# Modulation of a two-layer hybrid diffusion backbone: ring slots in column tiles of 512 columns, partial sums added by a selector

## The reference

```python
sh1, sc1, g1, sh2, sc2, g2 = jnp.split(jax.nn.silu(cv) @ w_mod + b_mod, 6, axis=-1)
h  = x * (1 + sc1) + sh1
z  = h @ w_in            # attention 512+128+128, mLSTM 4 x 256 + 16 gates, gMLP 2 x 256
y  = jnp.concatenate([att, m_out, g_out], axis=-1) @ w_out
x  = layer_norm(ALPHA * x + g1 * y, ln1_g, ln1_b)
h2 = x * (1 + sc2) + sh2
x  = layer_norm(ALPHA * x + g2 * (jnp.square(jax.nn.relu(h2 @ w_ff1)) @ w_ff2), ln2_g, ln2_b)
```

## Time and profile before

| what | us |
|---|---|
| median of the three runs shown (3286.88 to 3294.17) | 3290.51 |
| the profiled execution's own time | 3296.62 |
| its span | 3294.6 |
| PE busy in the span | 3089.8 (94%) |
| DVE busy | 1657.8 (50%) |
| ACT busy | 962.8 (29%) |
| POOL busy | 457.7 (14%) |
| mean granted clock of PE | 0.966 of 2.4 GHz |
| modulation slots from the ring | 160 of 256 KB, 2.9 to landing |
| chain that ended last | PE 83%, DVE 6%, issue 3%, DMA 3% |

### The profile page before, as it was taken

The page is one execution under the profiler, slowest core; times in us unless marked ns, Lnnn a source line. Parts: engine busy times, 40 slices in busy tenths (PEclk is TensorE's granted clock), DMA queues, the critical chain, the costliest instruction groups (busy, mean ns, idle before and its releaser), DMA issues.

```text
span 3294.6 us, 44616 instructions
## 1 busy us (share of the span) xinstructions
PE 3089.8 (94%) x17016; PEld 2540.1 (77%) x17016; DVE 1657.8 (50%) x3070; ACT 962.8 (29%) x1886; POOL 457.7 (14%) x600
## 2 busy tenths in 40 slices
PE   5999989998999999999968999899989999999996
PEld 4788845567888888889848888455668998899995
DVE  4447677747333333333484376777473333333337
ACT  3222344534221122111233223445342221212221
POOL 0012333412100000000020023334120000000003
PEclk8999989999999999999979999899999999999998
DMA  5440220022222222220321112200121111111113
GB/s 215 151 130 25 76 76 0 0 67 97 81 75 79 80 84 73 81 88 26 131 87 36 45 24 75 76 0 0 68 100 35 52 35 43 52 39 39 52 32 147
DMA packets 99368, 220.08 MB, mean 67 GB/s; under 512 B 13360, under 2 KB 13936, under 8 KB 98672
## 3 DMA queue, kind: packets, MB, share of 16 engines
q1 hardware_dynamic: 78240, 151.76, 14.6%
q0 software_dynamic: 20944, 65.80, 5.5%
HBM read 191.00 MB, written 26.51 MB: 66 GB/s over the span
## 4 chain that ended last, share of the span: by engine, by line
PE 83%; DVE 6%; issue 3%; DMA 3%; ACT 2%; POOL 1%; DVEq 1%; ACTq 1%; POOLq 1%; SPq 0%
PE ps L1655 22%; PE ps L1658 21%; PE ps L1659 21%; PE ps L1870 5%; PE ps L1841 3%; PE ps L1860 2%; PE ps L1637 2%; PE ps L1861 2%; DVE nm L1418 1%; PE ps L1768 1%; DMA w_raw<-in_w_slots 1%; DMA lnb<-in_ln_gb 1%; DVE w_lo L468 1%; POOLq L537 1%; PE ps L1763 1%
## 5 line engine op out<-in xcount | busy, mean ns | idle before, releaser
L1655 PE MATMUL ps<-hi,w_hi 128*128 128x384 f32 x1584 | 541.1, 342 | 29.4 <-DVEq L406 20.9
L1659 PE MATMUL ps<-hi,w_lo 128*128 128x384 f32 x1584 | 534.7, 338 | 0.0
L1658 PE MATMUL ps<-lo,w_hi 128*128 128x384 f32 x1584 | 534.1, 337 | 0.0
L1655 PE MATMUL ps<-w_hi,f_hi 128*128 128x512 f32 x1152 | 457.9, 397 | 19.4 <-DVE acc L1559 19.4
L1658 PE MATMUL ps<-w_lo,f_hi 128*128 128x512 f32 x1152 | 451.2, 392 | 0.0
L1659 PE MATMUL ps<-w_hi,f_lo 128*128 128x512 f32 x1152 | 450.3, 391 | 0.0
L463 ACT CAST w_hi<-w_raw 128x512 fp32r<-128x512 f32 x368 | 213.3, 619 | 763.9 <-PE ps L1655 716.3
L1559 DVE TENSOR_TENSOR acc<-acc,ps 128x512 f32<-128x512 f32 x288 | 196.2, 686 | 418.7 <-PE ps L1659 418.5
L1655 PE MATMUL ps<-w_hi,hi 128*128 128x512 f32 (+1 forms) x1008 | 388.8, 386 | 6.8 <-ACT stg L756 4.1
L1659 PE MATMUL ps<-w_hi,lo 128*128 128x512 f32 (+1 forms) x1008 | 380.7, 378 | 0.0
L1658 PE MATMUL ps<-w_lo,hi 128*128 128x512 f32 (+1 forms) x1008 | 380.5, 378 | 0.0
(11 more groups left out here) (277 smaller groups left out, 4106.5 us busy)
## 6 DMA issues: line engine op xcount, KB each, us to landing
w_raw<-in_w_slots SPq DMA_DIRECT2D x368, 256.0 KB, 3.3
w_raw<-in_m_slots SPq DMA_DIRECT2D x160, 256.0 KB, 2.9
x_dram<-xr POOLq DMA_DIRECT2D x18, 512.0 KB, 3.1
x1t<-x_dram POOLq DMA_DIRECT2D x6, 1536.0 KB, 14.9
out<-acc POOLq DMA_DIRECT2D x18, 512.0 KB, 3.0
modw<-in_w_mod SPq DMA_DIRECT2D x4, 2048.0 KB, 9.3
acc<-in_x_in SPq DMA_DIRECT2D x3, 1536.0 KB, 16.0
zq_dram<-stg POOLq DMA_DIRECT2D x18, 256.0 KB, 2.4
```

Source lines behind the costliest of these rows:

```text
L1655: mm = pe.matmul(out, a_hi, b_hi, start=first, stop=False)
L1658: pe.matmul(out, a_hi, b_lo, start=False, stop=False)
L1659: return pe.matmul(out, a_lo, b_hi, start=False, stop=last)
```

## The change

Seven edits go together.

1. **Slots in column tiles.** `mod_slots` takes four slots (in projection group 0 two) at a time, waits for all of them and makes one matmul of 512 columns for each, slot k in the strip of partitions 32 (k mod 4). A chunk is then four partial sums, each over two slots.
2. **Selector.** `mod_rows` copies the four strips, 2 x 512 each, to a row buffer; `mod_turn` is four matmuls with the 98 x 128 piece as the stationary side and a selector of two columns as the moving side, which turns and adds the four strips. Every chunk is turned, the gates too. The bias is loaded once as columns (`modbc`) and added in `mod_columns`.
3. **Gates.** Their columns go to `gcol`, one more matmul (`mod_gate`) turns them back into rows, DVE copies those (`mod_gates`), POOL stores them. The wait for those stores (mod_st) stands ahead of the next chunk's copies, from the first gate chunk on.
4. **Places.** Projection groups 0, 1, 2 take 2, 3, 3 chunks; group 0 visits after t = 0 to 7, groups 1 and 2 after t = 1 to 6, with turns after t = 3, 5, 7. In a first product PE visits after blocks 1 and 4, turns after 7, gates after 9; in a second after 4 and 8, 12, 15. DVE copies after hidden(6) or summed(9).
5. **Head.** Four buffers for w_mod, all requested at once; the x rows of tiles 0 to 2 ahead of the first weights, the others behind them; group 0's weights split after tiles 2 and 7, before after 5 and 8.
6. **First normalisation.** ACT applies mean and deviation in one pass (`normal1`); norm weight and bias are folded into the modulation columns (`mixed_columns`, `mixed`), so the transposes no longer wait for the weighted x. DVE weights x (`weighted1`, two passes) behind each of the first nine hidden blocks of piece 0, POOL stores it from there. POOL also forms nmean x rstd (`nbias`). PE's `x_turned` comes one tile sooner (t - 2).
7. **acc.** It is no longer cleared; the first piece copies into it.

The diff, cut to its core (the head's transfers, `mixed_columns`, places in memory and the acc edit are told above):

```diff
-Z_CHUNKS = {0: (0, 1, 2), 1: (3, 4), 2: (5, 6, 7)}
+Z_CHUNKS = {0: (0, 1), 1: (2, 3, 4), 2: (5, 6, 7)}
...
+        selm, gcol = condt[:, 0], sce[:, 0:4]
...
+                    deviation(2 * NT * L + t, t, True)
+                for i, t in enumerate(X1_ORDER):
+                    store1(i, t)
...
+                def normal1(t):
+                    act.wait_ge(S["ln_rstd"], 2 * NT * L + t + 1)
+                    act.activation(x_row(t), x_row(t), ACT.Identity, bias=nbias[:, t:t + 1], scale=rs[:, t:t + 1]).then_inc(S["xn_done"], 1)
+                act.wait_ge(S["mc_done"], L + 1)
                 for t in range(NT):
                     squares(2 * NT * L + t, t, x_row(t), sqr[:].rearrange("p (a b) -> p a b", b=W))
-                    if t == NT - 1:
-                        split_hi(act, L, 7, (S["o_out"], START + 18 * L + 18), range(RAW))
-                    if t >= 4:
-                        modulated(L, t - 4)
-                modulated(L, 5)
-                split_hi(act, L, 7, (S["o_out"], START + 18 * L + 18), range(RAW, SLOTS))
+                    if t:
+                        normal1(t - 1)
+                    if t >= 3:
+                        modulated(L, t - 3)
+                normal1(NT - 1)
                 for t in range(6, NT):
+                    if t < 8:
+                        split_hi(act, L, 7, (S["o_out"], START + 18 * L + 18), range((t - 6) * RAW, (t - 5) * RAW))
                     modulated(L, t)
...
             def mod_rows(m, bank):
                 dve.wait_ge(S["mod_ps"], KT * (m + 1))
-                if m < NCH:
-                    dve.wait_ge(S["mod_b0_ld"], 16)
-                else:
-                    dve.wait_ge(S["mod_b_ld"], 16 * (m - NCH + 1))
-                if m:
-                    before = [n for n in range(m) if kind_of(n) < 2]
-                    dve.wait_ge(S["mod_tp"], len(before))
-                    if kind_of(m - 1) == 2:
-                        dve.wait_ge(S["mod_st"], 64 * (m - len(before)))
-                own(dve)
-                b = modb0[:, m] if m < NCH else modb
+                dve.wait_ge(S["mod_tp"], m)
+                if m in (NCH, 3 * NCH):
+                    dve.memset(mod_place(m)[:], 0.0)
+                    dve.drain()
+                if gates_in(m):
+                    dve.wait_ge(S["mod_st"], 64 * gates_in(m))
                 for j in range(4):
                     r = slice(32 * j, 32 * j + 2)
-                    ins = dve.tensor_tensor(modr[r, :], ps[r, bank, m % NCH * P:(m % NCH + 1) * P], b[r, :], ALU.add)
+                    ins = dve.tensor_copy(mod_place(m)[r, :], ps[r, bank, :])
...
+                    src, b = ps[:, bank, 32 * j:32 * j + 2], modbc[:, 4 * m + j:4 * m + j + 1]
+                    if k == 2:
+                        ins = dve.tensor_scalar(gcol[:, j], src, b, None, ALU.add)
+                    elif j < 2:
+                        ins = dve.tensor_scalar(modc[:, o:o + 5:4], src, b, None, ALU.add)
                     else:
-                        ins = dve.tensor_scalar(modc[:, o:o + 5:4], src, 1.0, None, ALU.add)
+                        ins = dve.tensor_scalar(modc[:, o:o + 5:4], src, b, 1.0, ALU.add, ALU.add)
                 ins.then_inc(S["mod_col"], 1)
+            def mod_gates(m, bank):
+                dve.wait_ge(S["mod_gt"], gates_in(m + 1))
+                dve.tensor_copy(mod_place(m)[0:8, P:2 * P], ps[0:8, bank, P:2 * P]).then_inc(S["mod_gr"], 1)
...
+                modulation((NCH,))
+                modulation((NCH + 1,), True, False)
                 split_lo(dve, L, 1)
+                modulation((NCH + 1,), False)
...
-                for part in range(2):
-                    modulation(1, part)
+                modulation(range(NCH + 2, NCH + 5))
...
+                    if n == 1:
+                        modulation((NCH + 4,), False, False, True)
+                    if n in (4, 6, 8):
+                        modulation((NCH + 3 + n // 2,), False, False, True)
+                    if n in (2, 4, 6):
+                        modulation((NCH + 4 + n // 2,), True, False)
+                    if n in (3, 5, 7):
+                        modulation((NCH + 4 + n // 2,), False)
...
+                mixed_columns()
                 y_low(0)
                 y_low(1)
...
-                def normal1(t):
-                    normal(2 * NT * L + t, t, x_row(t), lnb, S["xr_done"])
+                def weighted1(t):
+                    dve.wait_ge(S["xT_ps"], 2 * NT * L + NT + t + 1)
+                    dve.tensor_tensor(x_row(t), x_row(t), w_row(lnb, 0), ALU.mult)
+                    dve.drain()
+                    dve.tensor_tensor(x_row(t), x_row(t), w_row(lnb, 1), ALU.add).then_inc(S["xr_done"], 1)
                 for t in range(NT):
                     residual(1, t)
                     negated_mean(t, mv[:, t, 0:1], mv[:, t, 1:2])
-                    if t == NT - 1:
-                        split_lo(dve, L, 7, range(RAW))
-                    if t:
-                        normal1(t - 1)
-                    if t >= 5:
-                        low2(t - 5)
                     if t >= 4:
-                        modulate2(L, t - 4)
-                low2(4)
-                modulate2(L, 5)
-                normal1(NT - 1)
-                low2(5)
-                modulate2(L, 6)
-                split_lo(dve, L, 7, range(RAW, SLOTS))
-                for t in range(7, NT):
+                        low2(t - 4)
+                    if t >= 3:
+                        modulate2(L, t - 3)
+                for t in range(6, NT):
+                    low2(t - 1)
                     modulate2(L, t)
-                    low2(t - 1)
+                    if t < 8:
+                        split_lo(dve, L, 7, range((t - 6) * RAW, (t - 5) * RAW))
                 low2(NT - 1)
...
                 def chunk(i):
                     for b in range(9):
                         hidden(i, b)
+                        if not i:
+                            weighted1(X1_ORDER[b])
+                        if b == 6:
+                            modulation(i, 0, 0)
                     split_lo(dve, L, 2 * i + 8, range(RAW))
                     hidden(i, 9)
-                    modulation(i, 0)
+                    modulation(i, 0, 1)
                     hidden(i, 10)
                     split_lo(dve, L, 2 * i + 8, range(RAW, SLOTS))
                     hidden(i, 11)
+                    modulation(i, 0, 2)
                 for i in range(NFF - 1):
                     chunk(i)
+                    if not i:
+                        dve.wait_ge(S["x1_st"], 16 * 7 * (L + 1))
+                        own(dve)
                     for b in range(14):
                         summed(i, b, True)
-                        if b == 10:
-                            modulation(i, 1)
+                        if b in (9, 13):
+                            modulation(i, 1, (9, 13).index(b))
                     split_lo(dve, L, 2 * i + 9, range(RAW))
                     for b in range(14, 17):
                         summed(i, b, True)
+                    modulation(i, 1, 2)
...
             def mod_slots(m, ks, bank):
-                c = m % NCH
-                if m and ks[0] == 0:
+                if m and not ks[0]:
                     pe.wait_ge(S["mod_row"], m)
                 for k in ks:
                     if m < NCH:
-                        src = modw[:, m % 2, k]
-                        pe.wait_ge(mod_w_ld[m % 2], 16 * (m // 2 + 1))
+                        pe.wait_ge(mod_w_ld[m], 16)
                     else:
-                        n = m * KT + k
-                        src = w_raw[:, AT["m", n] % RAW]
-                        pe.wait_ge(w_ld[AT["m", n] % RAW], landed("m", n))
-                    for j in range(4):
-                        mm = pe.matmul(ps[32 * j:32 * j + 2, bank, c * P:(c + 1) * P], sc[:, k, :], src[:, j * P:(j + 1) * P],
-                                       start=(k == 0), stop=(k == KT - 1))
-                    mm.then_inc(S["mod_ps"], 1)
+                        pe.wait_ge(w_ld[AT["m", m * KT + k] % RAW], landed("m", m * KT + k))
+                for k in ks:
+                    src = modw[m][:, k] if m < NCH else w_raw[:, AT["m", m * KT + k] % RAW]
+                    i = 32 * (k % 4)
+                    pe.matmul(ps[i:i + 2, bank, :], sc[:, k, :], src, start=k < 4, stop=k >= 4).then_inc(S["mod_ps"], 1)
             def mod_turn(m, bank):
                 pe.wait_ge(S["mod_row"], m + 1)
-                before = len([n for n in range(m) if kind_of(n) < 2])
-                if before:
-                    pe.wait_ge(S["mod_col"], before)
-                pe.transpose(ps[:, bank, 0:98], modr[0:98, :], ident[0:98, 0:98]).then_inc(S["mod_tp"], 1)
+                pe.wait_ge(S["mod_col"], m)
+                for j in range(4):
```

(46 more changed lines are left out.)

202 lines of the change are left out of this document (119 added, 83 removed).

## The result

The changed kernel takes **3309.5 us** (median of four runs, 3306.1 to 3312.0) against 3289.4 for the kernel before on the same chip: ratio 1.0058, 95% interval 1.0046 to 1.0071. It is 20 us slower; the forecast was 3286.6, the range ended at 3301. Between the two traces there are therefore only 9.7 us, and it is these that can be placed stage by stage.

A forecast was written before the change was run, and what follows sets the result against it. It took PE to bound projection groups and feed-forward, transfers the head, and PE not the first normalisation's tail. Terms summed to -3.9; 3296.6 (profiled execution) - 3.9 - 6.1 (to the median) = 3286.6 us; range 3268 to 3301.

The forecast's parts named there:

- The head: Start of the kernel, bounded by transfers: with four buffers loads follow each other, ACT starts at 32 to 34; -2.5 us.
- the clock's term: Four new PE waits of 3.3 us or more in groups 1, 2 and feed-forward bring half-speed time, 2.1 each: +8.5 us.
- Rival C: Each of the four waits costs 5.1 us of clock: 3298.5; sign, group 1 to 3 windows under 0.85; chance 0.16.
- Group 1: Projection group 1: PE waits 8.5 us for the second chunk's copies behind DVE's scan stage; group +12.9 us.
- Rival A: The waits in groups 1 and 2 do not arise, DVE being earlier or PE later: 3265.1; chance 0.12.
- Group 2: Projection group 2: turns, gates, later weight split and two waits of 3.3 us behind gate stores; +11.2 us.
- rival B: Short matmuls cost their issue alone, so a turn is 0.5 us: 3278.6; chance 0.10.
- E: Rival: the column tiles run one after another, a visit costs 4 x 0.86 us: over 3380; chance 0.02.
- Group 0: Projection group 0: eight visits of 1.0, one turn 0.9, 0.4 of waiting; 35.6 against 38.5, -2.9 us.
- First normalisation: Both layers: tail -18.7 us (22.7 against 30.6 and 30.0), following blocks -4.3, folded columns +2.0.
- Rival D: The normalisation's tail does not shorten because ACT becomes the bound, giving back 12 of 18.7: 3298.6; chance 0.10.
- Feed-forward: Remaining feed-forward products of layer 0: cheaper visits, less a 2.7 us gate wait in first products 4 and 5; -10.1 us.

The follow-up runs named there:

- experiments 1: Changed kernel with the head's chunks alternating between two PSUM banks and each turn behind the next chunk's matmuls: 3302.5 us, head 66.9.
- 3: Changed kernel with one copy of 98 partitions x 512 in place of four of 2 x 512, everywhere: 3283.4 us, ratio to before 0.9976.
- 4: Changed kernel with one copy of 98 partitions for the head's four chunks alone, four copies elsewhere: 3299.9 us, head 60.7.
- 2: Changed kernel with the head's loads requested in the order of the kernel before: 3312.5 us, ratio to before 1.0060, head 75.4.
- experiment 5: Changed kernel with unused matmuls added before each turn in the head: ten gave 3330.5 us (head 90.5), three gave 3303.2 us (head 67.5).
- experiment 7: Changed kernel with DVE copying group 1's first chunk inside the scan stage in place of after it: 3300.0 us.
- experiment 6: Changed kernel with the first three gate chunks' turned-back gates put in rows of wt, so copies don't wait for stores: 3299.0 us.

## Why the prediction was wrong

**The head, the step that failed.** The prediction costed it as transfers: "the fourth lands near 25.8", then two groups of four matmuls, the copies, the turn, "32 to 34: -2.5". That takes the first three chunks as done when the fourth lands. But each chunk's matmuls wait for the copies of the one before. They did so in the kernel before, where a chunk took 5.4 us, little more than a load. With copies grown from 1.18 to 2.79 and a longer turn the four chunks form a chain of 4 x 8.0 us, longer than the loads. The prices were in the text, and one chunk adds up to 5.4 us at full clock (1.7 + 2.8 + 0.9) and 7.2 with the matmuls at half clock; this sum was never set against the 4.9 us in which a load arrives. Measured +8.2, an error of 10.7 of the 13.4 between the traces (-3.9 against +9.5 by the table's sum); experiments 1, 3 and 4 undo it in three ways, 2 excludes the transfers.

The chain and the clock have unequal parts in the error. With the waits filled (experiment 5) a chunk takes 5.86 us, 1 us over the loads, and the head is 67.5, 3.9 over the 63.6 that the forecast gives (66.1 - 2.5). The other 7.1 us, to 74.6, are the half clock; ACT starts on its first tile at 37.5 and at 44.6. The head's term had the clock only as a range for the last chunk's matmuls, 1.7 to 3.5, and the clock's term counted no wait of the head, though the 2.8 of copies there are nearly the 3.3 that it counted elsewhere.

**The clock behind the waits.** Priced at 8.5 for groups 1 and 2 and the feed-forward. Groups 1 and 2 took 33.4 with it, against 24.1 + 8.5; so this held as a sum, though the share meant for the feed-forward (2.1) was not needed there. Its spread was real too: group 2, with the same two waits, took 3.4 us more in experiment 7. Rival C, as stated for the four waits of groups and feed-forward, falls by its own sign (the windows show 0.93 and 0.96, not under 0.85). Its mechanism is what slowed the head, where neither the forecast nor the rival had looked.

**Group 1.** A wait of 8.5 before the second chunk: measured 7.88, and experiment 7 confirms the cause. Rival A falls.

**Group 2.** Two waits of 3.3: 3.44 with DVE behind the gate stores, confirmed by experiment 6. The rest of the 17.5 is turns and gates as priced (3.7), half clock (0.04 x 81 = 3) and about 2.5 us where PE follows DVE's late split of the weights, priced at 1.1. The prediction's own terms add up to 11.4, not 11.2.

**Prices.** Visit 0.97, turn 0.92 to 0.99 at full clock (0.9), copies 2.79 (2.8). The rows of before bore all three; rival B falls, and so does E, whose visit would be 3.4; the overhead of 60 cycles that the Trainium skill gives each matmul (page TensorEngine Tiling (Array Packing), section Performance Considerations) would, as an estimate, make a turn of 8 records some 0.2 us; the measured 0.92 differs, and it decides. Group 0 gained 1.0 in place of 2.9: its last turn, 0.9, which I had put in group 1, stands in it, and its tiles go by at 3.07 where I took 2.9.

**First normalisation.** Predicted -21.0 (tail -18.7, blocks -4.3, columns +2.0), measured -16.5 in the traces and -9.6 by itself in the median. The tail is 24.3 and 24.3 in place of 30.6 and 30.0, not 22.7, and in both layers ACT waits 1.2 us in it for a weight slot to land:

```profile
856.08 1.24 ACT L487 CAST w_hi<-w_raw 128x512 fp32r<-128x512 f32 x2 [1.19 <-DMA w_raw<-in_w_slots]
```

The product's last tiles gave 0.5 a layer, where the recorded 18.7 comes out only with 1.7 a layer (7.9 + 7.3 + 2 x 1.7). Rival D, that the tail doesn't shorten, falls.

**Feed-forward.** -13.4 against -10.1. The failed term is the gate wait, priced at 2.7 in first products 4 and 5: PE waited 0.36. The second products gave less than priced (6.2 against 8.8; four times 1.7, besides, is 6.8 and not the 6.5 of the text).

```profile
1331.60 0.39 PE L1735 MATMUL ps<-ident,sce 128*8 128x128 f32 x2 [0.36 <-DVE sce L1070]
```

**From the profile to the median.** I took 6.1 off because the profiled execution of before lay so far above its median. That of the change lay 3.4 below its own. This is the other part of the miss: 9.5 of the 22.9 us, and no mechanism of the kernel is shown behind it. Where the scatter sits can be seen: from the start of layer 1's group 0 to its attention, which no edit touches, the fourteen traces show 324.3 to 331.4 us.

## What to carry to other kernels

When a chain of load, matmul, copy and turn repeats, add up one period of everything that is serial in it and compare it with the period of the loads before calling the stretch bound by transfers. Do it with the matmuls at half clock as well, since the waits of such a chain bring it: here 5.9 us a chunk became 8.0. Fewer, wider matmuls moved the cost to DVE: a copy is paid by its elements in the free dimension, so one over all the strips costs what one over two partitions does, and this single line was worth 26 us here. Look behind every new wait of PE for the half-speed time that follows it. Don't let the refill of a small buffer wait for the DMA store of what it held (group 2), nor for a long stage on the engine that empties it (group 1).

## What the hardware showed that I had not expected

- The order of output strips decides: ten matmuls of 512 columns into one strip took 8.7 us, 0.87 each, at full clock; eight spread over four strips took 1.71 to the next instruction, 0.21 each. The column tiles do run side by side, four times as fast.
- Waits of 3.0 us between stretches of 5 us of work went with a granted clock of 0.53 to 0.60; the same waits filled to 0.43 went with 1.00. Added work of 2.7 us a wait made the head 7.1 us shorter.
- The same pair of waits in group 2 is followed by a mean granted clock of 0.96 in one execution and 0.90 in another.
